# Two attention loops: the order of work within a unit on VectorE, and of value products and logits on TensorE

## The chip, the cores and the metric

The kernel runs on one core of one Trainium2 chip. The metric is the device time of one execution in microseconds (us); lower is better. PE is TensorE's matmul, PEld its weight load, DVE is VectorE, ACT is ScalarE, POOL is GpSimd and SP is SyncE.

## The reference, cut to what matters

The program is two blocks of two layers each, over 512 tokens of width 1024, with one mixer in each layer. Two of the four mixers are attention, and they are what the change touches: a sparse one in the first block ("dsa", two key and value heads) and a full one in the second ("attn", four key and value heads), both with 16 heads of 64 features and blocks of 128 queries. Everything else (the HGRN and Hyena mixers, the feed-forward stages) is unchanged.

```python
# dsa, for a block of 128 queries (keys after the query are masked out)
logits = jnp.einsum('btkgd,btskd->btkgs', qb, k_sel).astype(jnp.float32) * (ATT_HEAD_DIM ** -0.5)
logits = jnp.where(valid, logits + bias, NEG_BIG)
probs = jax.nn.softmax(logits, axis=-1)
out = jnp.einsum('btkgs,btskd->btkgd', probs, v_sel.astype(jnp.float32))

# attn, for a block of 128 queries
s = jnp.einsum('bqkgd,bskd->bkgqs', q_blk, k, preferred_element_type=jnp.float32) * scale
p = jax.nn.softmax(s, axis=-1).astype(v.dtype)
return jnp.einsum('bkgqs,bskd->bqkgd', p, v)
```

The kernel doesn't gather the selected keys of dsa. It works on all keys up to the end of the query block and adds a mask.

## The kernel before, in words

Each engine has a program of its own, written out in a fixed order. An engine runs its instructions strictly in that order; `wait_ge(*at(event))` holds it until the engine that makes the event has marked it. The two attention loops share one skeleton, `attend`, of which there is one version for each of PE, ACT and DVE; POOL runs `scale`.

The work is cut into 32 **units**, eight pairs of heads (j = 0 to 7) times four blocks of 128 queries (tt = 0 to 3). Unit u is pair j = u // 4 and block tt = u % 4, and each unit holds two heads (e = 0, 1). In attn every unit has 512 keys; in dsa a unit has 128 (tt + 1) keys, so 128, 256, 384 and 512. A unit passes through these steps:

1. PE, `logits(u)`: the product of queries and keys, one PSUM bank for each head (four banks, so units take turns by two). L942 in attn; L868 in dsa, followed by the mask, added by a product with the identity (L873).
2. DVE, `soften(u)`: the maximum over the keys of each head (L2023 in attn; in dsa L1939, which adds the bias in the same pass), then the negation of both maxima (L2026, L1943), which marks ("max", stage, u).
3. ACT, `soften(u, e)`: the exponential and its sum for each head (L1456, L1405).
4. DVE: the reciprocals of the two sums (L1877), marked ("rs", stage, u).
5. POOL: both heads' exponentials times the reciprocals (L2293).
6. PE, `turn(u)`: transposes in blocks of 128 x 128, head 0 into bank 4 and head 1 into bank 7 (L783). There is only one bank for each head: the transposes of unit u + 1 wait until those of unit u have been copied out.
7. ACT copies head 0's transposes (L1342) and DVE head 1's (L1884) into the tile `PT`, marked ("pt", stage, u, e). `PT` holds one pair of heads, so the copy of the first unit of a pair waits for the value products of the pair before.
8. PE, `values(j)`, once for each pair: the product with the values, 16 matmul records (L800), after the copies of all four units. Then ACT rounds the result (L1333) and DVE computes the low part (L1624), its `finish(j)`.

The steps are staggered. In turn i of the loop (`ALAG = 3`) PE makes the transposes of unit i - 3, then the logits of unit i, then in every fourth turn the value products of the pair that unit i - 4 completes. DVE makes the reciprocals of unit i - 1, the copy of unit i - 3, the maxima of unit i and in every fourth turn the low part. ACT makes the copy of unit i - 3, the exponentials of unit i and in every fourth turn the rounding. Turn i = 4j + 7 is the one with the value products of pair j, and unit 4j + 4, whose transposes are made in that turn, is the first of the next pair.

Of the kernel before, what the change touches and what calls it, by code (L numbers as in the profile page):

```python
# [241 lines left out]
class Signals:  # L242
# [6 lines left out]
    def mark(self, name, *events, by=1):  # L249
        self.total[name] = self.total.get(name, 0) + by  # L250
        for event in events:
            self.value[event] = (name, self.total[name])
        self.newest[name.split("_")[0]] = (name, self.total[name])
        return (self.handles[name] if self.handles else None), by
# [4 lines left out]
    def at(self, *event):  # L259
        if self.counted is None:  # L260
            return None, 0
        name, value = self.counted[event]
        return self.handles[name], value
# [85 lines left out]
def build(nc, A, out):  # L349
    ctx = ExitStack()  # L350
    with ctx:
# [144 lines left out]
        mark, at = signals.mark, signals.at  # L496
# [3 lines left out]
        def pe_program(pe):  # L500
            mark, at, end = signals.mark, signals.at, signals.end
            freed = [None] * 8

            def wait_bank(b):
                for event in freed[b] or ():
                    pe.wait_ge(*at(*event))
# [263 lines left out]
            def attend(stage, logits, value, M):  # L770

                units = UNITS[stage]
                n, sem = len(units), f"pe_{stage}"

                def turn(u):
                    keys = units[u][2]
                    for e in range(2):
                        b = TBANK[e]
                        pe.wait_ge(*at("scaled", stage, u, e))
                        wait_bank(b)  # L780
                        for s in range(keys // 128):
                            c = slice(128 * s, 128 * s + 128)
                            m = pe.transpose(ps[b][:, c], M.P[2 * (u % 4) + e][:, c], ident[:, :])  # L783
                        m.then_inc(*mark(sem, ("turned", stage, u, e)))
                        freed[b] = [("pt", stage, u, e)]

                def values(j):
                    b = OBANK[j % 2]
                    if j >= 2:
                        for part in ("hi", "lo"):  # L790
                            pe.wait_ge(*at("h", f"{stage}_o", j - 2, part))
                    else:
                        wait_bank(b)
                    for tt in range(4):
                        for e in range(2):
                            pe.wait_ge(*at("pt", stage, 4 * j + tt, e))
                    for s in range(4):
                        q0 = 128 * s if stage == "dsa" else 0
                        for e in range(2):
                            m = pe.matmul(ps[b][64 * e:64 * e + 64, q0:L], value(j, s), M.PT[e][:, s, q0:L], start=s == 0, stop=s == 3,  # L800
                                          skip_group_check=True)
                    m.then_inc(*mark(sem, ("value", stage, j)))

                for i in range(n + ALAG + 1):
                    if 0 <= i - ALAG < n:
                        turn(i - ALAG)
                    if i < n:
                        logits(i).then_inc(*mark(sem, ("logits", stage, i)))
                    u = i - ALAG - 1
                    if u >= 0 and u % 4 == 3:  # L810
                        values(u // 4)
                for j in (6, 7):
                    freed[OBANK[j % 2]] = [("h", f"{stage}_o", j, "hi"), ("h", f"{stage}_o", j, "lo")]

            def dsa():
# [45 lines left out]
                def logits(u):  # L861
# [10 lines left out]
                    for e in range(2):  # L872
                        m = pe.matmul(ps[logit_bank(u, e)][:, 0:keys], S.ident[:, :], S.masked[tt], start=False, stop=True)  # L873
                    return m

                pe.wait_ge(*at("dv"))
                attend("dsa", logits, lambda j, s: S.V[:, s, 64 * (j // 4):64 * (j // 4) + 64], S)
                residual("pe_dsa", 5, [("dsa", "out", j) for j in range(4)], ((2, 3), (4, 5)),
                         lambda k: [("h", "dsa_o", k, "hi"), ("h", "dsa_o", k, "lo")])
# [9 lines left out]
            def attention():  # L889
# [56 lines left out]
                for tt in range(4):  # L946
                    pe.wait_ge(*at("av", tt))
                attend("attn", logits, lambda j, s: T.V[:, s, 64 * (j // 2):64 * (j // 2) + 64], T)
                residual("pe_attn", 10, [("attn", "out", j) for j in range(4)], ((2, 3), (4, 5)),
                         lambda k: [("h", "attn_o", k, "hi"), ("h", "attn_o", k, "lo")])  # L950
# [646 lines left out]
        def dve_program(dve):  # L1597
            mark, at, end = signals.mark, signals.at, signals.end
# [23 lines left out]
            def low(dst, src, high, sem, name):  # L1622
                dve.wait_ge(*at(*name, "hi"))
                dve.tensor_tensor(dst, src, high.bitcast(F), SUB).then_inc(*mark(sem, (*name, "lo")))  # L1624
# [239 lines left out]
            def attend(stage, M, soften):  # L1864
                units = UNITS[stage]
                n, sem = len(units), f"dve_{stage}"

                def finish(j):
                    low(hl[:, j, :], ps[OBANK[j % 2]][:, :], hh[:, j, :], "dve_h", ("h", f"{stage}_o", j))

                for i in range(n + ALAG + 1):
                    u = i - 1
                    if 0 <= u < n:
                        c = slice(2 * (u % 4), 2 * (u % 4) + 2)
                        for e in range(2):
                            dve.wait_ge(*at("exp", stage, u, e))
                        dve.reciprocal(M.rs[:, c], M.sm[:, c]).then_inc(*mark(sem, ("rs", stage, u)))  # L1877
                    u = i - ALAG
                    if 0 <= u < n:
                        j, tt, keys = units[u]  # L1880
                        dve.wait_ge(*at("turned", stage, u, 1))
                        if j:
                            dve.wait_ge(*at("value", stage, j - 1))
                        dve.tensor_copy(M.PT[1][:, 0:keys // 128, 128 * tt:128 * tt + 128],  # L1884
                                        ps[TBANK[1]][:, 0:keys].rearrange("p (s q) -> p s q", q=128)).then_inc(*mark(sem, ("pt", stage, u, 1)))
                    if i < n:
                        soften(i)
                    u = i - ALAG - 1
                    if u >= 0 and u % 4 == 3:
                        finish(u // 4)  # L1890

            def dsa(before):
# [40 lines left out]
                def soften(u):  # L1933
# [9 lines left out]
                    dve.tensor_scalar(S.nm[:, c:c + 2], S.mx[:, c:c + 2], -1.0, None, MUL).then_inc(*mark("dve_dsa", ("max", "dsa", u)))  # L1943

                attend("dsa", S, soften)
                residual(5, ((2, 3), (4, 5)), [("dsa", "out", j) for j in range(4)])
                end("dve", "dsa")
# [29 lines left out]
            def attention(before):  # L1977
# [41 lines left out]
                def soften(u):  # L2019
# [6 lines left out]
                    dve.tensor_scalar(T.nm[:, c:c + 2], T.mx[:, c:c + 2], -0.125, None, MUL).then_inc(*mark("dve_attn", ("max", "attn", u)))  # L2026

                attend("attn", T, soften)
                residual(10, ((2, 3), (4, 5)), [("attn", "out", j) for j in range(4)], scale_of("attn"))
                end("dve", "attn")  # L2030
# [492 lines left out]
```

## Time and profile before

| what | value |
|---|---|
| time before, median of 3 runs | 3147.76 us (3147.2 to 3148.05) |
| the profiled execution's own time | 3144.56 us |
| its span | 3142.8 us |
| PE busy | 2874.8 us (91%) |
| DVE busy | 1794.6 us (57%) |
| ACT busy | 1017.5 us (32%) |
| POOL busy | 325.4 us (10%) |
| dsa loop | about 975 to 1101 us |
| attn loop | about 1672 to 1827 us |

The span runs from the first to the last instruction of the profiled execution. The shares are means over the whole program, most of which is dense matmuls in front of which no other engine stands; the two loops together are 280 us of it, with a mix of their own.

### The profile page before, as it was taken

What the parts mean: (1) busy time and instruction counts of PE and PEld (TensorE: products, weight loads), DVE (VectorE), ACT (ScalarE), POOL (GpSimd) and SP (SyncE); (2) the same over time, 40 slices, a digit from 0 to 9 for tenths busy, and PEclk for the clock granted to TensorE, in tenths of its full rate; (3) what the DMA queues carried; (4) which work ended last, traced back from release to release, by engine and by line L of the source; (5) the groups of instructions that cost most, each with busy time, mean ns of one, the idle gap of its engine ahead of it and who ended that gap; (6) DMA issues with size and microseconds to landing.
All of it is one profiled execution on the core that took longest, in us unless ns stands there. A gap on an engine that the chain in (4) does not pass through costs nothing.

```text
span 3142.8 us, 33865 instructions
## 1 busy us (share of the span) xinstructions
PE 2874.8 (91%) x13568; PEld 2308.3 (73%) x13568; DVE 1794.6 (57%) x2550; ACT 1017.5 (32%) x1366; POOL 325.4 (10%) x271
## 2 busy tenths in 40 slices
PE   7988789999997799999997789999998988899999
PEld 6777678888774478888783367888777777678887
DVE  3277746565576437474545536564655798554433
ACT  3223224242333434242424423232332233332322
POOL 0000000000001200000202310000000677200000
PEclk9999889999997899999898989999999688999999
DMA  5710114443322024343320015454421000322221
GB/s 141 154 41 27 41 54 144 134 133 112 89 67 68 21 77 141 121 141 97 102 67 14 1 54 163 155 174 133 140 81 44 26 18 22 111 78 94 95 86 47
DMA packets 260436, 275.67 MB, mean 88 GB/s; under 512 B 23159, under 2 KB 229495, under 8 KB 260280
## 3 DMA queue, kind: packets, MB, share of 16 engines
q1 hardware_dynamic: 230088, 218.44, 22.8%
q10 hardware_dynamic: 30192, 55.05, 5.6%
q8 instruction: 109, 1.79, 0.3%
q14 instruction: 47, 0.39, 0.0%
HBM read 266.13 MB, written 7.34 MB: 87 GB/s over the span
## 4 chain that ended last, share of the span: by engine, by line
PE 75%; DVE 14%; ACT 5%; issue 3%; DMA 1%; SPq 1%; POOL 0%; ACTq 0%; DVEq 0%; POOLq 0%
PE ps L515 21%; PE ps L517 21%; PE ps L516 21%; DVE sb L1615 2%; PE ps L800 2%; DVE sb L1642 2%; PE ps L665 1%; PE ps L558 1%; DMA sb<-in_hgrn_w_in 1%; PE ps L567 1%; PE ps L783 1%; PE ps L979 1%; ACT sb L1456 1%; DVE sb L2023 1%; DVE sb L2156 1%
## 5 line engine op out<-in xcount | busy, mean ns | idle before, releaser
L515 PE MATMUL ps<-sb 128*128 128x512 f32 (+1 forms) x3552 | 1364.6, 384 | 93.2 <-DVE sb L1648 18.8
L516 PE MATMUL ps<-sb 128*128 128x512 f32 (+1 forms) x3552 | 1347.4, 379 | 0.0
L517 PE MATMUL ps<-sb 128*128 128x512 f32 (+1 forms) x3552 | 1347.3, 379 | 0.0
L515 PEld LDWEIGHTS ps<-sb 128*128 128x128 f32 x3552 | 687.4, 194 | 248.6 <-issue 68.5
L517 PEld LDWEIGHTS ps<-sb 128*128 128x128 f32 x3552 | 687.1, 193 | 125.0
L516 PEld LDWEIGHTS ps<-sb 128*128 128x128 f32 x3552 | 688.1, 194 | 119.1 <-issue 0.7
L1615 DVE TENSOR_TENSOR sb<-sb 128x2048 fp32r<-128x2048 f32 (+2 forms) x198 | 446.6, 2256 | 372.2 <-ACT sb L1130 372.1
L1130 ACT ACTIVATE sb<-sb 128x2048 fp32r<-128x2048 f32 (+2 forms) x198 | 368.7, 1862 | 291.2 <-PE ps L517 272.5
L1800 DVE SCALAR_TENSOR_TENSOR sb<-ps,sb 128x511 f32<-128x511 f32 (+1 forms) x264 | 197.7, 749 | 190.2 <-ACT sb L1288 184.0
L2261 POOL TENSOR_TENSOR sb<-sb 128x512 f32<-128x512 f32 x45 | 62.1, 1387 | 1714.0 <-ACT sb L1167 1712.0
L1288 ACT ACTIVATE sb<-ps,sb 128x512 f32<-128x512 f32 x132 | 100.1, 774 | 304.9 <-PE ps L517 304.9
L783 PE MATMUL ps<-sb 128*128 128x128 f32 x416 | 75.7, 326 | 65.4 <-ACT sb L1342 62.2
L1675 DVE SCALAR_TENSOR_TENSOR sb<-ps,sb 128x512 f32<-128x512 f32 x64 | 46.3, 751 | 153.8 <-PE ps L517 153.6
L1820 DVE SCALAR_TENSOR_TENSOR sb<-sb 128x512 f32<-128x512 f32 x168 | 126.0, 750 | 12.9 <-DVE sb L1817 0.5
L783 PEld LDWEIGHTS ps<-sb 128*128 128x128 f32 x416 | 56.4, 167 | 102.7 <-issue 96.8
L2293 POOL TENSOR_SCALAR sb<-sb 128x512 f32<-128x512 f32 (+3 forms) x128 | 76.7, 612 | 485.7 <-DVE sb L1877 485.7
L1673 DVE TENSOR_TENSOR sb<-sb,ps 128x512 f32<-128x512 f32 x64 | 43.5, 687 | 127.4 <-PE ps L517 127.2
L1315 ACT ACTIVATE sb<-sb 128x512 fp32r<-128x512 f32 x88 | 55.3, 633 | 180.1 <-DVE sb L1842 108.5
L1167 ACT ACTIVATE sb<-sb 128x512 f32<-128x512 f32 x72 | 45.0, 642 | 206.0 <-DVE sb L1675 108.9
L1300 ACT ACTIVATE sb<-sb 128x512 f32<-128x512 f32 x88 | 55.6, 632 | 137.1 <-DVE sb L1800 137.1
L665 PEld LDWEIGHTS ps<-sb 128*128 128x128 f32 x512 | 72.6, 210 | 28.9 <-issue 23.6
L665 PE MATMUL ps<-sb 128*128 128x128 f32 x512 | 75.2, 295 | 18.8 <-DVE sb L1721 18.8
(213 smaller groups left out, 2354.2 us busy)
## 6 DMA issues: line engine op xcount, KB each, us to landing
sb<-in_ffn_w_up SPq DMA_DIRECT2D x88, 1024.0 KB, 5.1
sb<-in_ada_w ACTq DMA_DIRECT2D x192, 256.0 KB, 3.2
sb<-in_ffn_w_down SPq DMA_DIRECT2D x32, 1024.0 KB, 5.0
sb<-in_ffn_w_down SPq DMA_DIRECT2D x16, 768.0 KB, 4.3
sb<-in_hy_w_in SPq DMA_DIRECT2D x12, 1024.0 KB, 5.1
sb<-in_hgrn_w_in SPq DMA_DIRECT2D x8, 1024.0 KB, 11.1
sb<-in_hgrn_w_in SPq DMA_DIRECT2D x16, 512.0 KB, 5.5
sb<-in_dsa_w_in SPq DMA_DIRECT2D x6, 1024.0 KB, 5.3
```

The source lines that it names most:

```text
L515: pe.matmul(o, al, bh, start=f, stop=False, **kw)
L516: pe.matmul(o, ah, bl, start=False, stop=False, **kw)
L517: m = pe.matmul(o, ah, bh, start=False, stop=l, **kw)
L665: m = pe.matmul(ps[bk][:, c], a_[:, c], b_[:, c], start=True, stop=True)
L783: m = pe.transpose(ps[b][:, c], M.P[2 * (u % 4) + e][:, c], ident[:, :])
L800: m = pe.matmul(ps[b][64 * e:64 * e + 64, q0:L], value(j, s), M.PT[e][:, s, q0:L], start=s == 0, stop=s == 3, skip_group_check=True)
L1130: act.activation(wh[w][:, 0:n], raw[it["r"]][:, 0:n], ACTF.Copy).then_inc(*mark("act_hi", ("hi", it["key"])))
L1288: act.activation(dst[:, :], ps[b][:, :], ACTF.Identity, bias=bias(tile), scale=wt(offset, tile)).then_inc(*mark("act_ffn", (name + "_0", n ...
L1615: dve.tensor_tensor(wl[w][:, 0:n], raw[it["r"]][:, 0:n], wh[w][:, 0:n].bitcast(F), SUB).then_inc(*mark("dve_lo", ("lo", it["key"])))
L1800: dve.scalar_tensor_tensor(o, i, cv[0](tap, tile), o, MUL, ADD).then_inc(*mark("dve_ffn", (name, n, tile) if last else (name + "_1", n, ti ...
L1820: m = dve.scalar_tensor_tensor(a, w[:, :], cact[:, f:f + 1], a, MUL, ADD)
L2293: pool.tensor_scalar(P, P, M.rs[:, c:c + 1], 1.0, MUL, MUL).then_inc(*mark(f"pool_{stage}", ("scaled", stage, u, e)))
```

## The change

Two pieces of code change places, one in PE's `attend` and one in DVE's. No instruction is added, removed or altered, and ACT, POOL and SP run what they ran before, in the same order. Two lines move in each place:

```diff
 # PE, attend
                 for i in range(n + ALAG + 1):
                     if 0 <= i - ALAG < n:
                         turn(i - ALAG)
-                    if i < n:
-                        logits(i).then_inc(*mark(sem, ("logits", stage, i)))
                     u = i - ALAG - 1
                     if u >= 0 and u % 4 == 3:
                         values(u // 4)
+                    if i < n:
+                        logits(i).then_inc(*mark(sem, ("logits", stage, i)))
 # DVE, attend
                 for i in range(n + ALAG + 1):
+                    if i < n:
+                        soften(i)
                     u = i - 1
                     if 0 <= u < n:
...
                         dve.tensor_copy(M.PT[1][:, 0:keys // 128, 128 * tt:128 * tt + 128],
                                         ps[TBANK[1]][:, 0:keys].rearrange("p (s q) -> p s q", q=128)).then_inc(*mark(sem, ("pt", stage, u, 1)))
-                    if i < n:
-                        soften(i)
                     u = i - ALAG - 1
                     if u >= 0 and u % 4 == 3:
                         finish(u // 4)
```

On DVE, in the attn loop around a turn with `finish` (L1624), these rows stood before. L2023 is a unit's two maxima, L2026 their negation, L1877 the reciprocals, L1884 the copy of head 1's transposes.

```order
1373 L1624 TENSOR_TENSOR sb<-ps,sb 128x512
1374 L1877 RECIPROCAL sb<-sb 128x2
1375 L1884 COPY sb<-ps 128x4x128
1376 L2023 TENSOR_REDUCE sb<-ps 128x1 x2
1377 L2026 TENSOR_SCALAR sb<-sb 128x2
1378 L1877 RECIPROCAL sb<-sb 128x2
1379 L1884 COPY sb<-ps 128x4x128
1380 L2023 TENSOR_REDUCE sb<-ps 128x1 x2
1381 L2026 TENSOR_SCALAR sb<-sb 128x2
```

At the same place of the changed kernel, where the reciprocals are L1879 and the copy L1886, stands this.

```order
1372 L1886 COPY sb<-ps 128x4x128
1373 L1624 TENSOR_TENSOR sb<-ps,sb 128x512
1374 L2023 TENSOR_REDUCE sb<-ps 128x1 x2
1375 L2026 TENSOR_SCALAR sb<-sb 128x2
1376 L1879 RECIPROCAL sb<-sb 128x2
1377 L1886 COPY sb<-ps 128x4x128
1378 L2023 TENSOR_REDUCE sb<-ps 128x1 x2
1379 L2026 TENSOR_SCALAR sb<-sb 128x2
```

Reciprocals and copy still stand between one unit's negation and the next one's maxima, but they belong to a unit earlier: behind the maxima of unit i came the reciprocals of unit i and the copy of unit i - 2, and now come the reciprocals of unit i - 1 and the copy of unit i - 3. Only after L1624 do the maxima now follow at once.

On PE, in the attn loop, this is one piece of the difference, around a turn with value products (L800); L783 are the eight transposes of a unit and L942 its logits.

```order
 L942 MATMUL ps<-sb 128x512 x2
 L783 MATMUL ps<-sb 128x128 x8
+L800 MATMUL ps<-sb 64x512 x8
 L942 MATMUL ps<-sb 128x512 x2
-L800 MATMUL ps<-sb 64x512 x8
 L783 MATMUL ps<-sb 128x128 x8
 L942 MATMUL ps<-sb 128x512 x2
```

The value products move ahead of the logits of the same turn, and stay behind that turn's transposes; the dsa loop has the same move. The other three turns in four are as they were on PE.

## Rows read from the trace of the kernel before

**Rows 1.** Busy time by stretch: the dsa loop, then the attn loop.
```profile
core 0: us, PE busy (x) PEld busy (x) DVE busy (x) ACT busy (x) POOL busy (x), PEclk, DMA share, GB/s
975.40:1101.20 125.80, 99.55 (x468) 56.44 (x468) 55.91 (x232) 52.69 (x167) 33.21 (x64) 0.81 0.11 34
1672.20:1826.70 154.50, 111.45 (x514) 51.55 (x513) 74.19 (x169) 65.97 (x167) 43.47 (x64) 0.90 0.00 1
```

**Rows 2.** Timeline, one plain attn unit: start, length, engine [idle before].
```profile
1744.30 0.17 DVE L2026 TENSOR_SCALAR sb<-sb 128x2 f32<-128x2 f32 x1
1744.51 0.69 ACT L1456 ACTIVATE sb<-ps,sb 128x512 f32<-128x512 f32 x1 [2.34 <-DVE sb L2026]
1746.06 0.17 DVE L1877 RECIPROCAL sb<-sb 128x2 f32<-128x2 f32 x1 [1.58 <-ACT sb L1456]
1746.14 0.67 DVE L1884 COPY sb<-ps 128x512 f32<-128x512 f32 x1
1746.58 1.07 PE L783 MATMUL ps<-sb 128*128 128x128 f32 x8 [0.26 <-ACT sb L1342]
1746.72 1.28 DVE L2023 TENSOR_REDUCE sb<-ps 128x1 f32<-128x512 f32 x2
1747.58 1.13 PE L942 MATMUL ps<-sb 64*128 64x512 f32 x4
1748.04 0.17 DVE L2026 TENSOR_SCALAR sb<-sb 128x2 f32<-128x2 f32 x1
```

**Rows 3.** Timeline, attn turns with value products and with the low part.
```profile
1739.55 0.17 DVE L2026 TENSOR_SCALAR sb<-sb 128x2 f32<-128x2 f32 x1
1741.72 0.69 DVE L1624 TENSOR_TENSOR sb<-ps,sb 128x512 fp32r<-128x512 f32 x1 [2.00 <-ACT sb L1333]
1742.40 0.67 DVE L1884 COPY sb<-ps 128x512 f32<-128x512 f32 x1
1743.22 1.08 PE L783 MATMUL ps<-sb 128*128 128x128 f32 x4 [0.28 <-DVE sb L1884]
1744.23 2.08 PE L942 MATMUL ps<-sb 64*128 64x512 f32 x4
...
1752.37 3.65 PE L800 MATMUL ps<-sb 128*64 128x512 f32 x16
```

**Rows 4.** Timeline, dsa: units of 512 and of 128 keys.
```profile
1055.12 1.13 PE L868 MATMUL ps<-sb 64*128 64x512 f32 x4
1056.17 0.73 PE L873 MATMUL ps<-sb 128*128 128x512 f32 x2
1056.84 2.38 PE L800 MATMUL ps<-sb 128*64 128x512 f32 x16
1059.54 0.68 DVE L1939 CUSTOM_DVE_ANT_0 sb<-ps,sb 128x512 f32<-128x512 f32 x1
1060.28 0.49 PE L868 MATMUL ps<-sb 64*128 64x128 f32 x4
1060.70 0.44 PE L873 MATMUL ps<-sb 128*128 128x128 f32 x2
1060.87 0.17 DVE L1943 TENSOR_SCALAR sb<-sb 128x2 f32<-128x2 f32 x1
```

**Rows 5.** Timeline: first and last of 32 negations, attn, then dsa.
```profile
1674.74 0.17 DVE L2026 TENSOR_SCALAR sb<-sb 128x2 f32<-128x2 f32 x1
1813.70 0.17 DVE L2026 TENSOR_SCALAR sb<-sb 128x2 f32<-128x2 f32 x1
976.02 0.17 DVE L1943 TENSOR_SCALAR sb<-sb 128x2 f32<-128x2 f32 x1
1091.93 0.17 DVE L1943 TENSOR_SCALAR sb<-sb 128x2 f32<-128x2 f32 x1
```

**Rows 6.** Timeline, PE alone: the transposes that end the dsa loop.
```profile
1094.54 3.49 PE L783 MATMUL ps<-sb 128*128 128x128 f32 x14 [3.12 <-ACT sb L1342]
```

**Rows 7.** Busy time by stretch, right behind them (columns as in rows 1).
```profile
1098.00:1099.00 1.00, 0.12 (x3) 0.13 (x4) 0.69 (x1) 0.00 (x0) 0.00 (x0) 1.00 0.00 0
```

## The prediction

> **What bounds the kernel now.** The page says that PE is busy for 91% of the span, but a change to two loops has to be read from the loops. The busy time by stretch [rows 1] gives them: PE is busy 99.6 of 125.8 us in dsa and 111.5 of 154.5 us in attn, at mean granted clocks of 0.81 and 0.90, so neither PE nor any other engine fills them. What sets the pace is a ring of waits, which the timeline of one plain attn unit shows [rows 2]. The negation starts at 1744.30 and releases ACT's exponentials (1744.51). When both are done DVE, idle for 1.58 us, takes the reciprocals (1746.06), then the copy (1746.14), the maxima (1746.72) and the next negation (1748.04). One unit is 3.74 us, a ring of DVE and ACT alone. PE is beside it: its eight transposes start at 1746.58 and its logits at 1747.58, and those are the logits for the next maxima but one to start, well over a microsecond later. PE makes a unit's logits while DVE waits for ACT.
>
> In the turn with value products, DVE's and ACT's copies wait for those (L800, 3.65 us [rows 3]), and in the next turn the low part comes first: L1624 starts 2.17 us behind the negation at 1739.55 and the next negation is at 1744.30, a unit of 4.75 us. From the first negation to the last, 31 steps, attn takes 138.96 us and dsa 115.91 us [rows 5].
>
> **What the change takes away.** DVE now takes the maxima of unit i before the reciprocals of unit i - 1, so the reciprocals wait for exponentials that began a whole unit earlier. The wait of 1.58 us goes.
>
> **What it puts there.** The copy behind a negation is now that of unit i - 3, where it was unit i - 2 (seen from the negation of unit i). Bank 7 holds one unit's transposes, so PE's transposes of head 1 wait for that copy, and the next logits stand behind these transposes in PE's order. The next maxima wait for those logits. So there is a new ring, of DVE and PE: copy, transposes of head 1, logits, maxima, negation, reciprocals, copy. Nothing in it overlaps. ACT is out of it; head 0's transposes are too, since ACT's copy is made earlier.
>
> Its length for a plain attn unit, with PE at 2.4 GHz: negation to copy 0.19 (0.08 from reciprocals to copy [rows 2], and about 0.11 for the negation, an estimate from its record of 0.17). The copy's record is 0.67 and PE starts 0.15 after it (1742.40 + 0.67, then 1743.22 [rows 3]). Four transposes are half of the 1.00 us between the starts 1746.58 and 1747.58, so 0.50. The logits' record is 1.13 and I add 0.04 to the start of DVE. Maxima to negation is 1.32 (1746.72 to 1748.04). The sum is 0.19 + 0.67 + 0.15 + 0.50 + 1.17 + 1.32 = **4.00 us against 3.74**. The ring that goes was the shorter one.
>
> The turn with value products: they now stand between transposes and logits, so they lie on the ring whole: 4.00 + 3.55 (3.65 less the overlap with the next matmul, an estimate) = 7.55 us. Here the PE edit counts against the kernel, since DVE asks for the logits first and needs the value products only for the copy behind them. The turn after it is bound by the low part: negation to low part 2.17 [rows 3], its slot 0.60, maxima 1.32, together 4.09 us (0.60 is 1742.40 less 1741.72, less the 0.08 of the reciprocals between them). That is 0.66 less than 4.75, the reciprocals and the copy being out of the way. A group of four units is 4.00 + 4.00 + 7.55 + 4.09 = 19.64 us. Before it was 18.4: three start-up steps of 3.74 us, two of them without the copy's 0.59, are 10.0, and 138.96 less 10.0 over 7 groups is 18.4.
>
> At the start of the loop there is a gain. Until unit 3 nothing is turned, and those three steps of 10.0 us take about 6.5, an estimate: unit 1 costs DVE only 1.32 + 0.1, since its logits are ready, and units 2 and 3 wait for a bank that the exponentials of unit 0 and 1 free, some 2.5 us each. So attn at 2.4 GHz is 6.5 + (4.00 x 3 + 7.55) + 6 x 19.64 = 143.9 us, **5 us more** than 138.96.
>
> The same for dsa by number of keys [rows 4]. Logits with mask are 1.78 us for 512 keys (1055.12 to 1056.17 + 0.73) and 0.86 for 128, so 1.16 and 1.47 between; maxima to negation 1.33 for 512 (1059.54 to 1060.87) and for 128 an estimate of 0.54, so 0.80 and 1.07; copies 0.67 down to an estimate of 0.29 (for both a quarter of the part that goes with the keys, over a fixed part of 0.28 and 0.16); transposes of head 1 0.125 for each 128 keys, and they are those of the following unit; value products 2.25. With 0.38 of fixed steps each unit is: 256 keys 0.38 + 0.42 + 0.38 + 1.16 + 0.80 = 3.14; 384 keys 0.38 + 0.54 + 0.50 + 1.47 + 1.07 = 3.96; 512 keys 0.38 + 0.67 + 0.13 + 2.25 + 1.78 + 1.33 = 6.54; the 128-key unit, bound by the low part, 3.4. A group is 17.0 us. With 5.5 for the start, 15.9 for units 4 to 7 and six groups it is 123.4 us, **7.5 us more** than 115.91 (of which today's low clock is already part).
>
> **The clock.** So far PE ran at 2.4 GHz. In the old ring PE's speed was hidden: in rows 3 four transposes took 1.08 us and logits 2.08 where rows 2 have 1.13, at half the clock, and the next unit was still 3.74 us later. In the new ring it isn't. On the path PE has per attn group about 8.2 + 1.5 us, per dsa group 7.3 us, and at 1.2 GHz these double: 29.3 against 19.64 us, 24.3 against 17.0. And the clock should be low more often. The loops already run at 0.90 and 0.81 [rows 1]; in the plain attn unit PE now works 2.2 of 3.74 us, later 2.2 of 4.00, with its pause grown from about 1.55 to 1.8 us. Bounds: at 2.4 GHz throughout nothing is added; at 1.2 GHz throughout 7.5 groups x 9.7 = 73 us in attn and 7.5 x 7.3 = 55 us in dsa. I take mean clocks of 0.77 and 0.70, each somewhat more than ten points below today's. With 46% of the time low, 36% of attn's work is done at the low clock (0.46 x 19.64 over 0.46 x 19.64 + 0.54 x 29.3), which is 0.36 x 73 = 26 us; with 60% low it is 51% in dsa, 28 us.
>
> **Sum:** 5 + 7.5 + 26 + 28 = 66.5 us, rounded down to 64 for what today's measured dsa loop already pays in its tail behind the last negation. The profiled execution was 3144.56 us and would be 3209; the median of the runs stands 3.2 above that execution, so 3147.8 + 64 = **3212 us**.
>
> One row bears on how the clock returns. Behind the last dsa negation PE had only transposes: 14 in 3.49 us, 0.25 each against 0.13 at the full clock, so at 1.2 GHz [rows 6]. Right behind them the granted clock is 1.00 [rows 7], so transposes alone brought it back, and the next plain units, which are half transposes, can do the same. The Trainium skill, page "TensorE: Matmul & The Clock Gate", section on the PE-mode transpose, says that transposes don't count as busy for the clock. By that rule the new loops would stay low much longer, toward the bound of 1.2 GHz throughout. This trace disagrees with it.
>
> **The rivals.**
>
> *The clock holds* (0.14). PE's pauses grow by only a quarter of a microsecond in plain attn units, and most of those kept 2.4 GHz. Then only the rings count, 12.5 us, with up to 20 more if today's mean clocks stay: 3160 to 3180 us. These are 3147.8 + 12.5 and + 32.5.
>
> *The clock stays low through both loops* (0.08). The new pauses, and plain units half of whose work is transposes, keep PE at 1.2 GHz. 12.5 + 128 is 3288 us if complete; with value products bringing it back each time, 3240 to 3288. The Trainium skill's rule on transposes, named above, leads here. Against it speak the transposes that brought the clock back [rows 6, 7], and at the low clock PE works 4.3 of 5.6 us, a larger share than now.
>
> *Faster: the new ring doesn't close* (0.04). If PE had the logits ready when DVE asks, the unit would be DVE's own work, 0.19 + 0.59 + 1.32 = 2.1 us, or PE's own 2.2. Groups would be about 12.5 us in attn and 11 in dsa, some 40 and 25 us less: about 3080 us. It decides at 3.74 us: were the sum of copy, four transposes, logits and maxima below that, attn would gain. My sum is 4.00, of which 0.34 are estimates of gaps, and the order on PE (transposes of unit i - 3, then logits of unit i) leaves no way around it.
>
> *No change* (0.02): a ring just at 3.74 us with the start-up gains, and a clock that rises.
>
> **How the numbers follow.** The forecast has 0.72, with its own range of 3188 to 3236 us (mean clocks five to eight points either side). Together with the upper part of the held clock and the lower part of the low one, 3178 to 3238 holds 8 in 10. 0.2% is 6.3 us, about what a measurement tells from no change. Faster 0.04, same 0.02, slower 0.94.
>
> **What would show it.** DVE's wait before the reciprocals (L1879) goes, and a wait before the maxima (L2023, L1939) on PE's logits takes its place, about 1.8 us in each plain attn unit. A plain attn unit at full clock is 4.0 us and one with value products 7.5. The granted clock falls to about 0.77 and 0.70. ACT no longer stands on the chain that ended last. It is wrong if logits are ready when DVE gets to the maxima, and off by tens of microseconds if the clock in the two loops stays where it is.

## The result, and the profile after

The changed kernel takes **3200.33 us** (median of 4 runs, 3195.96 to 3206.71) against 3147.91 in the same series: the ratio is 1.016, with a 95% interval of 1.0146 to 1.0174. It is 52 us slower; forecast were 64, in a range of 3178 to 3238 us. The profiled execution took 3206.71 us, at the slow end of its own runs, with a span of 3204.9 us against 3142.8.

The page of the changed kernel has these two lines:

```profile
span 3204.9 us, 33851 instructions
PE 2908.2 (91%) x13568; PEld 2318.5 (72%) x13568; DVE 1792.1 (56%) x2550; ACT 1017.5 (32%) x1366; POOL 325.5 (10%) x271
```

DVE, ACT and POOL do the same work in the same time. PE has as many instructions (13568), and is busy 33 us longer: the same matmuls ran slower. The count of all instructions is 14 lower (33851 against 33865), though nothing was taken out of the text and no engine's count on the second line changed; the kernel with VectorE's edit alone has 33851 too, so it comes with that edit. Busy time by stretch, each from a loop's first negation to its last, dsa and attn (the columns are those of [rows 1]):

```profile
978.20:1135.80 157.60, 115.83 (x436) 59.11 (x436) 50.87 (x220) 49.39 (x159) 30.73 (x60) 0.65 0.09 27
1721.00:1876.60 155.60, 107.25 (x468) 46.31 (x468) 67.84 (x157) 62.33 (x159) 40.74 (x60) 0.89 0.00 1
```

For the kernel before, the same stretches have 115.9 us and a granted clock of 0.81, and 139.0 us and 0.93. So dsa is 41.7 us longer and attn 16.6; the 3.8 us left of the 62 in the spans lie outside these stretches.

The timeline of the changed kernel, one plain attn unit at full clock (1.00 in this stretch), from negation to negation (to be read against [rows 2]):

```profile
1756.22 0.17 DVE L2026 TENSOR_SCALAR sb<-sb 128x2 f32<-128x2 f32 x1
1756.30 0.17 DVE L1879 RECIPROCAL sb<-sb 128x2 f32<-128x2 f32 x1
1756.38 0.67 DVE L1886 COPY sb<-ps 128x512 f32<-128x512 f32 x1
1757.20 0.63 PE L783 MATMUL ps<-sb 128*128 128x128 f32 x4 [1.77 <-DVE sb L1886]
1757.75 1.13 PE L942 MATMUL ps<-sb 64*128 64x512 f32 x4
1758.81 0.66 PE L783 MATMUL ps<-sb 128*128 128x128 f32 x4
1758.93 1.29 DVE L2023 TENSOR_REDUCE sb<-ps 128x1 f32<-128x512 f32 x2 [1.88 <-PE ps L942]
1760.25 0.17 DVE L2026 TENSOR_SCALAR sb<-sb 128x2 f32<-128x2 f32 x1
```

The wait of 1.58 us before the reciprocals is gone: they follow the negation by 0.08. In its place PE's four transposes wait 1.77 us for the copy, and DVE's maxima 1.88 us for the logits. The eight transposes of a unit have come apart: the four of head 0, at 1758.81, run ahead right behind the logits, and the four of head 1 wait for bank 7. One turn of the ring is 4.03 us.

The same view of the turn with value products, and of the turn behind it:

```profile
1740.46 0.17 DVE L2026 TENSOR_SCALAR sb<-sb 128x2 f32<-128x2 f32 x1
1742.00 3.65 PE L800 MATMUL ps<-sb 128*64 128x512 f32 x16
1745.59 1.13 PE L942 MATMUL ps<-sb 64*128 64x512 f32 x4
1746.76 1.29 DVE L2023 TENSOR_REDUCE sb<-ps 128x1 f32<-128x512 f32 x2 [5.46 <-PE ps L942]
1748.09 0.17 DVE L2026 TENSOR_SCALAR sb<-sb 128x2 f32<-128x2 f32 x1
1750.26 0.69 DVE L1624 TENSOR_TENSOR sb<-ps,sb 128x512 fp32r<-128x512 f32 x1 [1.34 <-ACT sb L1333]
1750.87 1.28 DVE L2023 TENSOR_REDUCE sb<-ps 128x1 f32<-128x512 f32 x2
1752.18 0.17 DVE L2026 TENSOR_SCALAR sb<-sb 128x2 f32<-128x2 f32 x1
```

The first is 7.63 us, with DVE idle for 5.46 us while value products and logits pass. The second is 4.09 us, set by the low part.

At half the clock (0.50 while they run) the logits look like this, 2.08 us where they were 1.13, and DVE waits for them:

```profile
1774.26 2.08 PE L942 MATMUL ps<-sb 64*128 64x512 f32 x4
1776.38 1.29 DVE L2023 TENSOR_REDUCE sb<-ps 128x1 f32<-128x512 f32 x2 [3.29 <-PE ps L942]
```

The waits of the whole loops, who waited for whom, in total, times and longest; attn (three lines), then dsa:

```profile
DVE sb L2023 <- PE ps L942: 79.3, 28, 7.2
ACT sb L1456 <- DVE sb L2026: 71.2, 31, 6.7
PE ps L783 <- DVE sb L1886: 46.8, 29, 2.1
...
DVE sb L1939 <- PE ps L873: 94.5, 24, 7.2
ACT sb L1405 <- DVE sb L1943: 92.2, 31, 11.2
PE ps L783 <- DVE sb L1886: 32.8, 23, 2.2
```

DVE waits for PE's logits, and PE's transposes for DVE's copy: two engines that wait for each other in turn. The first of these waits is there in 28 (attn) and 24 (dsa) of the 32 units. On the chain of work that ended last, ACT's exponentials fall from about 24% to under 4% of the time between attn's first and last negation, and from about 10% to 4% in dsa. They don't leave it altogether, as the prediction had it. Between a negation and the low part behind it the chain still runs through them.

### The profile page after: what moved, and what is told of

It reads as the page before. It is cut to its first block, busy times and chain, and to the rows that moved or that the text cites. A ratio compares the mean times of both kernels' runs of the same rounds, so it can differ in the third digit from the quotient of the medians.

```text
span 3204.9 us, 33851 instructions
## 1 busy us (share of the span) xinstructions
PE 2908.2 (91%) x13568; PEld 2318.5 (72%) x13568; DVE 1792.1 (56%) x2550; ACT 1017.5 (32%) x1366; POOL 325.5 (10%) x271
## 4 chain that ended last, share of the span: by engine, by line
PE 76%; DVE 15%; ACT 3%; issue 3%; DMA 1%; SPq 1%; POOL 0%; ACTq 0%; DVEq 0%; POOLq 0%
PE ps L515 21%; PE ps L517 20%; PE ps L516 20%; PE ps L800 2%; DVE sb L1615 2%; DVE sb L1642 1%; PE ps L665 1%; PE ps L558 1%; PE ps L783 1%; PE ps L979 1%; DMA sb<-in_hgrn_w_in 1%; DVE sb L2023 1%; PE ps L567 1%; PE ps L942 1%; PE ps L868 1%
## 5 line engine op out<-in xcount | busy, mean ns | idle before, releaser
L783 PE MATMUL ps<-sb 128*128 128x128 f32 x416 | 88.9, 341 | 93.6 <-DVE sb L1886 79.6
L783 PEld LDWEIGHTS ps<-sb 128*128 128x128 f32 x416 | 57.2, 170 | 142.2 <-issue 112.4
L665 PE MATMUL ps<-sb 128*128 128x128 f32 x512 | 75.0, 295 | 18.7 <-DVE sb L1721 18.6
```

The costliest lines, as they stand in the source:

```text
L665: m = pe.matmul(ps[bk][:, c], a_[:, c], b_[:, c], start=True, stop=True)
```

## The experiments

**VectorE's edit alone.** TensorE's order is put back.

```diff
                         turn(i - ALAG)
+                    if i < n:
+                        logits(i).then_inc(*mark(sem, ("logits", stage, i)))
                     u = i - ALAG - 1
                     if u >= 0 and u % 4 == 3:
                         values(u // 4)
-                    if i < n:
-                        logits(i).then_inc(*mark(sem, ("logits", stage, i)))
```

> VectorE's order is the new one, TensorE's the old one. Theory of the ring (copy, transposes of head 1, logits, maxima): the ring is closed by VectorE's edit alone, since the copy that frees bank 7 is made a unit later. Plain attn units are 4.0 us here too, the value products (3.6 us) are partly covered again by the maxima, and TensorE's clock is lower than before the change in dsa. Expected 3170 to 3190 us, so somewhat less than half of the change's 52 us gone. Rival, that it is TensorE's edit that costs (the value products ahead of the logits): then this kernel is at or below 3148 us.

Measured: 3190.83 us (3185.10 to 3195.16), ratio 1.0129 (1.0114 to 1.0145). The ring is there with this edit alone: plain attn units at full clock take 4.03 us, with the same wait for the logits.

```profile
1735.95 0.17 DVE L2026 TENSOR_SCALAR sb<-sb 128x2 f32<-128x2 f32 x1
1738.66 1.29 DVE L2023 TENSOR_REDUCE sb<-ps 128x1 f32<-128x512 f32 x2 [1.88 <-PE ps L942]
1739.98 0.17 DVE L2026 TENSOR_SCALAR sb<-sb 128x2 f32<-128x2 f32 x1
```

The edit brings 41 us of the 52, and the rival falls. From first to last negation the loops are 139.2 us at 0.73 (dsa) and 150.9 us at 0.83 (attn). The time is just above the range expected, with the low clock also in attn.

**TensorE's edit alone.** VectorE's order is put back (shown against the changed kernel).

```diff
                 for i in range(n + ALAG + 1):
-                    if i < n:
-                        soften(i)
                     u = i - 1
...
+                    if i < n:
+                        soften(i)
                     u = i - ALAG - 1
```

> TensorE's order is the new one, VectorE's the old one. Theory of the ring: with VectorE's old order the maxima of a turn with value products come after the copy, which waits for the value products, so these should come first on TensorE; a gain of 0.6 us in each such turn, seven of each loop, less what the clock takes back: 3140 to 3147 us. Rival, that TensorE's edit is what costs: 7 x 3.6 us in each loop, about 3190 us.

Measured: 3143.79 us (3142.49 to 3146.99, 10 runs), ratio 0.9981 (0.9972 to 0.9990). By itself this edit is a small gain, as the ring has it: most attn units with value products take 5.61 us instead of 6.28, and from first to last negation attn takes 4.1 us less and dsa 3.1. Beside VectorE's edit it costs 9.5 us (3200.33 less 3190.83, medians of two series). The sign of the one edit depends on the other.

**Logits ahead of the transposes.** VectorE as in the change.

```diff
                 for i in range(n + ALAG + 1):
+                    if i < n:
+                        logits(i).then_inc(*mark(sem, ("logits", stage, i)))
                     if 0 <= i - ALAG < n:
                         turn(i - ALAG)
                     u = i - ALAG - 1
                     if u >= 0 and u % 4 == 3:
                         values(u // 4)
-                    if i < n:
-                        logits(i).then_inc(*mark(sem, ("logits", stage, i)))
```

> VectorE's order is the new one; TensorE makes in each turn the logits, then the transposes, then the value products. Logits of unit i wait no longer for the copy of unit i - 4. Theory of the ring: this opens it, a plain attn unit falls from 4.0 us to between 2.3 and 3 us, and the kernel is 3070 to 3090 us, 60 to 80 us below the one before the change. Rival, that VectorE's new order is bad in itself (late reciprocals make GpSimd's scaling and the transposes late): it stays above 3148 us.

Measured: **3081.13 us** (3078.17 to 3085.00), ratio 0.9782 (0.9766 to 0.9798), the fastest version of this study, 69 us below the kernel before in the same series (3149.82 us). The ring is open. The loops, dsa and attn from first to last negation, in busy time by stretch of this kernel:

```profile
976.80:1062.30 85.50, 76.82 (x424) 43.22 (x426) 52.47 (x219) 49.21 (x158) 30.90 (x60) 0.93 0.17 50
1649.70:1749.90 100.20, 89.27 (x450) 43.55 (x452) 67.06 (x158) 61.15 (x158) 40.95 (x60) 0.98 0.00 1
```

A plain attn unit is 2.1 us, which is what DVE itself works: 1.28, 0.17, 0.17 and 0.67 us of records, which overlap a little, without a wait between them. In its timeline:

```profile
1686.03 0.17 DVE L2026 TENSOR_SCALAR sb<-sb 128x2 f32<-128x2 f32 x1
1686.11 0.17 DVE L1879 RECIPROCAL sb<-sb 128x2 f32<-128x2 f32 x1
1686.19 0.67 DVE L1886 COPY sb<-ps 128x512 f32<-128x512 f32 x1
1686.78 1.28 DVE L2023 TENSOR_REDUCE sb<-ps 128x1 f32<-128x512 f32 x2
1688.09 0.17 DVE L2026 TENSOR_SCALAR sb<-sb 128x2 f32<-128x2 f32 x1
...
1697.25 0.69 DVE L1886 COPY sb<-ps 128x512 f32<-128x512 f32 x1 [3.11 <-PE ps L800]
```

The rival, that late reciprocals do harm, falls. What is left is the turn with value products, in which the copy waits 3.11 us for them; the wait falls into the step from this turn's negation to the next one, which takes 7.7 us with the low part.

**The same order on TensorE, VectorE's order as before the change.**

> TensorE makes logits, then transposes, then value products; VectorE's order is the old one, so the ring of VectorE and ScalarE (exponentials, reciprocals, copy, maxima, 3.74 us) sets the pace again. Expected about 3130 us (3122 to 3142): a small gain from units around the value products. Then VectorE's edit, which costs 41 us under the old order of TensorE, is worth 40 to 60 us under this one. Rival, that TensorE's order alone makes the gain of 69 us: near 3081 us here too.

Measured: 3138.71 us (3134.94 to 3139.88), ratio 0.9961 (0.9947 to 0.9974). Plain attn units are 3.73 us, the old ring of DVE and ACT. The gain of about 9 us is dsa's alone: from first to last negation dsa takes 102.7 us instead of 115.9, and attn 143.3 instead of 139.0. So in dsa the old order on TensorE cost time even before the change, which the prediction, with its ring of DVE and ACT for an attn unit, doesn't have. And VectorE's edit, 41 us the wrong way under one order on TensorE, is worth 58 us (3138.71 less 3081.13) under the other.

**Only the waiting transposes behind the logits.** VectorE as in the change.

```diff
-                        turn(i - ALAG)
+                        turn(i - ALAG, (0,))
+                    if i < n:
+                        logits(i).then_inc(*mark(sem, ("logits", stage, i)))
+                    if 0 <= i - ALAG < n:
+                        turn(i - ALAG, (1,))
                     u = i - ALAG - 1
                     if u >= 0 and u % 4 == 3:
                         values(u // 4)
-                    if i < n:
-                        logits(i).then_inc(*mark(sem, ("logits", stage, i)))
```

`turn(u, heads)` makes the transposes of the heads named.

> VectorE's order is the new one; in each of TensorE's turns come the transposes of head 0, the logits, the transposes of head 1, the value products. Only the transposes that wait for VectorE's copy (bank 7) stand behind the logits; those that wait for ScalarE's copy (bank 4) stay ahead of them. Theory, that the ring is closed by VectorE's copy and bank 7 alone: the time is within 15 us of the 3081 us of the kernel with all transposes behind the logits. Rival, that transposes ahead of the logits cost through ScalarE's copy as well: it stays above 3120 us.

Measured: 3091.06 us (3088.13 to 3094.26), ratio 0.9810 (0.9792 to 0.9829), 10 us above the kernel with all transposes behind. It is the transposes of head 1, those that wait for VectorE's copy, that close the ring. With those of head 0 left ahead of the logits only 10 us of the gain are missing (12 if each kernel is held against the one before the change in its own series).

**The clock, with work in the pause.** To keep TensorE busier, if possible without lengthening the ring, the changed kernel gets a product that nothing uses, in the pause before the transposes of head 1.

```diff
+                def keep_busy(i):
+                    j = max(0, (i - 7) // 4 + 1)
+                    b = OBANK[j % 2]
...
+                    jj, tt, keys = units[i]
+                    q, k = (M.q, M.k2[:, jj // 4, :]) if stage == "dsa" else (M.q, M.kr[:, jj // 2, :])
+                    pe.matmul(ps[b][:, 0:keys], q[0:64, jj, 128 * tt:128 * tt + 128], k[0:64, 0:keys], start=True, stop=True)
...
                     if i < n:
                         logits(i).then_inc(*mark(sem, ("logits", stage, i)))
+                    if ALAG <= i < n:
+                        keep_busy(i)
```

> The changed kernel with one more product at the end of each of TensorE's turns from the fourth on, of the same operands as the unit's first logits (0.2 to 0.5 us at full clock), into the output bank that the next value products will overwrite; its result is used by nothing. It lies in the pause in which TensorE waits for VectorE's copy. Theory that the low clock is about two thirds of the loss: the granted clock in both loops rises above 0.9 and the time falls from 3200 to 3160 to 3170 us, although TensorE does more work. Rival, that the low clock only shows idleness and costs nothing: the time stays at 3200 us or rises.

Measured: 3197.23 us (3195.28 to 3202.28), ratio 1.0153 (1.0138 to 1.0168). The expected time was missed and the total says nothing, but the stages do. In attn the granted clock was 1.00 and the 31 units took 145.2 us instead of 155.7; after the start all but one of them took 4.03, 7.62 or 4.09 us, to 0.01. In dsa, where the product is only as wide as the unit has keys, the clock was 0.71 and the units took 155.7 us instead of 157.6. There the product didn't stay in the pause:

```profile
1035.28 1.65 PE L814 MATMUL ps<-sb 64*128 64x384 f32 x2
```

At the low clock it takes 1.65 us in a 384-key unit, and that unit took up to 5.84 us where the changed kernel has 5.57. So the attn loop answers the question and the dsa loop of this run doesn't.

Two wider products in dsa, of 512 columns whatever the keys:

> The changed kernel with longer unused products in TensorE's pause: two of 512 columns in each dsa turn (about 1 us at full clock), one in each attn turn as before. With the short ones attn ran at a granted clock of 1.00 and its 31 units took 145.2 us instead of 155.7, but dsa stayed at 0.71 and 155.7. Theory that the low clock is most of dsa's loss: its clock rises above 0.85 and its 31 units take 125 to 135 us, the kernel 3160 to 3175 us. Rival, that TensorE needs more than its pause for them: the clock stays low and the kernel is above 3200 us.

Measured: 3170.62 us (3164.07 to 3175.17), ratio 1.0061 (1.0038 to 1.0084). Both loops in busy time by stretch, dsa and attn:

```profile
977.60:1110.30 132.70, 132.39 (x550) 61.26 (x550) 50.70 (x219) 50.42 (x159) 30.72 (x60) 0.98 0.11 32
1693.20:1838.50 145.30, 118.14 (x526) 52.27 (x526) 67.68 (x158) 62.25 (x159) 40.75 (x60) 1.00 0.00 1
```

More work, and 30 us less time than the changed kernel. In dsa PE is busy without a pause now, and the 384-key unit is 4.59 us, so the two products overrun there. One product of 512 columns in each turn of both loops:

> The changed kernel with one unused product of 512 columns in each turn of both loops. The long ones (two in dsa) raised dsa's clock to 0.98 and shortened its 31 units from 157.6 to 132.7 us, but the traces show that one takes TensorE 0.9 us, not the 0.5 assumed, so that two overran the pause of the 384-key unit (4.59 us instead of 3.96). Theory: one fits, the 384-key unit falls to about 4.0 us, dsa's 31 units to 126 to 131 us and the kernel to 3158 to 3168 us, unless one is too little to hold the clock, in which case dsa stays at 150 us or more and the kernel above 3185 us.

Measured: 3166.38 us (3164.35 to 3178.63), ratio 1.0055 (1.0037 to 1.0072). The 384-key unit is 3.98 us. The profiled execution lost its clock in one dsa group (0.91 in the mean), whose units show both levels side by side: 4.31, 6.69 and 9.12 us for 256, 384 and 512 keys, against 3.15, 3.98 and 6.69 in most of the others. dsa took 133.6 us with that group, above the 126 to 131 expected; with a group of 17.2 us in its place it would be 127. The kernel's time is inside its range.

The two products in the kernel before the change:

> The kernel before the change with the same unused products. In the old ring of VectorE and ScalarE, TensorE's speed is hidden in plain units, so a higher clock should give little: attn stays within 2 us of 139, dsa between 112 and 118 us for its 31 units, the kernel 3142 to 3152 us. If the low clock cost as much here as in the changed kernel, it would fall by 10 us or more.

Measured: 3164.04 us (3161.34 to 3166.69), ratio 1.0051 (1.0032 to 1.0069). In attn the clock rose from 0.93 to 0.96 and the 31 units took 140.8 us against 139.0: a higher clock buys nothing there. The groups say it more sharply: in the last six the clock was 1.00 and each took 18.50 us, and in the kernel before these six took 18.5 to 18.6 at clocks between 0.82 and 1.00. In dsa they took 131.4 us. That is no answer on the clock, since the products overran PE's pause and made PE the bound, 4.55 us in the 384-key unit; the expected 112 to 118 us for dsa, and with it 3142 to 3152 us for the kernel, were missed for that reason.

## Why the prediction was right, step by step

**The ring of DVE and PE** was forecast at 4.00 us for a plain attn unit, 7.55 with value products and 4.09 with the low part; at full clock they are 4.03, 7.63 and 4.09. Of the terms, the four transposes are 0.55 us and not 0.50 (1757.20 to 1757.75), and the negation is 0.08 and not 0.11. For dsa 3.14, 3.96, 6.54 and 3.4 stand against 3.15, 3.98, 6.69 and 3.38, in the kernel with one product of 512 columns in the pause. That it is this ring is shown by opening it: with the logits ahead of the transposes the units are 2.1 us, and moving head 1's transposes alone gives 57 us of the gain of 69.

**The loss at full clock** was forecast at 5 us in attn and 7.5 in dsa. Attn with its clock held took 145.2 us, 6.3 more than before. For dsa no run held the clock throughout; the start (7.6 us instead of the 5.5 estimated, at half the clock), then 16.2 and six groups of 17.2 us give 127, 11 more than before. Of the 3.6 us that this is above the forecast 123.4, the start has 2.1. How much of these is the low clock and how much the estimate stays open, since no run has the start of dsa at full clock. In attn the start was as estimated, 6.52 us against 6.5.

**The clock** was the term with the widest bounds, and it was mis-sized in attn. I took mean clocks of 0.77 and 0.70 and costs of 26 and 28 us. They were 0.89 and 0.65, and the costs are 155.7 - 145.2 = 10.5 us in attn and 157.6 - 127 = 31 us in dsa. What was mis-sized is the assumption "each somewhat more than ten points below today's": from first to last negation attn fell by four points and dsa by sixteen. The price was right: the prediction's own formula gives 12 us for 0.89 in attn and 34 us for 0.65 in dsa. Why dsa lost so much more of its clock isn't settled: the pauses of TensorE differ with the number of keys there, and no run varied them by themselves. That the low clock is a cost on this path, and no mere sign of idleness, the products in the pause show; that it was hidden in the old attn ring is shown by the groups of that loop, 18.6 us at a clock of 0.82 and 18.5 at 1.00.

**The sum.** 6 + 11 + 10.5 + 31 is 59 us, of the 62 between the two profiled executions; 3.8 lie outside these stretches. Forecast were 66.5, rounded to 64. That the sums come so near each other is in part luck: 15.5 us too much for attn's clock stand against 3 too little for dsa's, nearly 5 too little for the rings and 3.8 for which there was no term. The medians differ by only 52, because the profiled execution of the changed kernel is the slowest of its four, 6.4 us above their median, and the one of the kernel before is 3.4 below its own. So the loops' shares hold for a slow execution; for the median they were not taken apart. The spread of 11 us fits a loop in which each stretch at the low clock lengthens the path; that link was not tested.

**TensorE's edit** was put at the whole of the value products, 3.55 us in each such unit, and called a loss beside VectorE's edit. The sign held (plus 9.5 us); that without VectorE's edit it is a gain (6 us) was expected before that run, not in the prediction. As what the edit costs, 3.55 us a group is much too high: with VectorE's edit alone the unit with value products takes 4.04 us at full clock, but the copy behind its negation then waits 2.0 us for them and the next unit takes 6.69, together 10.7 against 7.63 + 4.09 = 11.7. That is 1 us a group in attn. In the profiled executions the two kernels differ by 4.7 us in attn and by 18.3 in dsa, where the clock was 0.73 and 0.65; how much of dsa's difference is the clock was not taken apart.

**The rule on transposes** (the Trainium skill, "TensorE: Matmul & The Clock Gate", section on the PE-mode transpose: they don't count as busy for the clock) would have kept the loops low. Attn at a mean of 0.89, with transposes for nearly half of TensorE's work in plain units, fits this trace's disagreement with it but doesn't decide it, since the other half are logits, every fourth unit has value products, and dsa stayed at 0.65, lower than forecast. The clear evidence against it is [rows 6, 7], where PE had transposes alone. The profile lists these as MATMUL and names no mode.

**The rivals.** With the clock held 3160 to 3180 us were forecast, and that is where the two kernels with a nearly held clock are (medians 3166 and 3171). Both do the unused products besides, so this is no clean measurement of it. The faster case needed the logits to be there when DVE asks, which is what the logits-first order does: 3081 us, where 3080 stood for it, with 39 us less in attn and 30 in dsa where 40 and 25 were put.

## What to carry to other kernels

A wait that is moved on one engine is only gone if what then comes first has been made ready by the engine that makes it: follow the new order once round, through every buffer that an operation frees, and add up the ring that it closes before counting the wait as saved. Order the producing engine first, since the same edit on VectorE cost 41 us or brought 58, by what stood ahead of the logits on TensorE. And if a change puts TensorE on the path with a pause in every unit, price its half clock: in the old attn ring a group took 18.5 to 18.6 us at mean clocks from 0.82 to 1.00, and in the new one units at the low level cost 10.5 us of attn's 156 and about 31 of dsa's 158.

## What the runs showed of the hardware that was not expected

A product over 64 rows alone takes longer by the column than the two heads' logits do together. In the timeline of the changed kernel with the long unused products, PE alone:

```profile
1740.80 1.13 PE L957 MATMUL ps<-sb 64*128 64x512 f32 x4
1741.76 1.02 PE L815 MATMUL ps<-sb 64*128 64x512 f32 x2
```

Four records of the logits (L957, rows 0 to 63 and 64 to 127, two banks) take 0.96 us to the start of the next matmul (1740.80 to 1741.76), 0.24 each. The two records of the unused product (L815, rows 0 to 63 only) start 0.43 us apart: 1.02 us, less the 0.59 of a single one. The logits' records overlap in pairs. In narrower stretches of the same trace the first two run together from 1740.80 for 0.70 us, and the other two from 1741.33 for 0.60.

The Trainium skill has this in "TensorEngine Tiling (Array Packing)", section Key Properties: different tiles can execute their weight loads and matmuls in parallel. This trace agrees for the two halves of the rows, but no run here separates rows from banks. So one unused product of 512 columns takes about 0.9 us where 0.5 was assumed; one fitted the pause of the 384-key unit in dsa (3.98 us) and two did not (4.59).

And products that nothing uses made a kernel 34 us faster (3200.33 to 3166.38): the mean granted clock went from 0.65 to 0.91 in dsa and from 0.89 to 0.99 in attn.
